# The order of VectorE's steps around rotary rows and score factors, and two buffers for the expert activations, in an encoder layer on one core

## The reference, cut to what matters

```python
def encoder_layer(x, ...):               # x_prompt (1,256,1024) and x_sample (1,512,1024), f32
    h = rms_norm(x, norm1_g)
    proj = h @ w_in                      # six slices of 512 columns and 32 low-rank columns
    gq, gk, gv, gog, glr_f, glr_b, dq, dk, dv = split(proj)
    a = gla_mixer(...)                   # 4 heads, chunked gated linear attention, forward and backward
    d = diff_attention(...)              # 4 heads; q = apply_rope(rms_norm(q)), k likewise
    x = x + concat(a, d) @ w_out
    h2 = rms_norm(x, norm2_g)
    return x + expert_choice_ffn(h2, ...)  # 16 experts, each takes its own 2*n/16 tokens

def apply_rope(x):                       # first half times cos minus second times sin, and so on
    return concatenate([x1*cos - x2*sin, x2*cos + x1*sin], axis=-1)

# gated linear attention, one head and direction, b the running sum of the log gates in a chunk of 64
scores = (q * exp(b - b_mid)) @ (k * exp(b_mid - b)).T     # masked, then times v

# one expert: xe its rows, 2048 hidden columns
ye = (silu(xe @ w_gate) * (xe @ w_up)) @ w_down * gates
out[idx] += ye
```

## Time and profile before

| | us |
|---|---|
| median of 3 runs | 1541.56 (1541.54 to 1542.34) |
| the profiled execution's own time | 1541.64 |
| its span | 1539.8 |
| PE busy | 1503.8 (98%) |
| DVE busy | 1242.6 (81%) |
| ACT busy | 1089.9 (71%) |
| POOL busy | 123.3 (8%) |

### The profile page before, as it was taken

The page is one execution under the profiler, slowest core; times in us unless marked ns, Lnnn a source line. Parts: engine busy times, 40 slices in busy tenths (PEclk is TensorE's granted clock), DMA queues, the critical chain, the costliest instruction groups (busy, mean ns, idle before and its releaser), DMA issues.

```text
span 1539.8 us, 18601 instructions
## 1 busy us (share of the span) xinstructions
PE 1503.8 (98%) x7293; PEld 1228.2 (80%) x7293; DVE 1242.6 (81%) x1133; ACT 1089.9 (71%) x1230; POOL 123.3 (8%) x103
## 2 busy tenths in 40 slices
PE   7999999999989999999999999999999999999997
PEld 6787777678868888888888888888888888888885
DVE  5348678785589898888889888888988888898985
ACT  7456356775457778787777878778777878778784
POOL 1023131000000101000000000010000101000000
PEclk9999999999999999999999999999999999999999
DMA  6111101401759999999999999999999999999992
GB/s 232 56 55 56 38 18 56 152 28 56 273 182 390 367 385 378 395 381 393 376 386 387 376 394 379 393 380 385 384 377 393 379 394 379 387 389 382 393 370 66
DMA packets 191942, 447.98 MB, mean 291 GB/s; under 512 B 12968, under 2 KB 13296, under 8 KB 191856
## 3 DMA queue, kind: packets, MB, share of 16 engines
q1 hardware_dynamic: 187440, 433.03, 75.3%
q0 software_dynamic: 3968, 12.65, 3.5%
q10 hardware_dynamic: 448, 1.12, 0.2%
HBM read 434.19 MB, written 12.58 MB: 290 GB/s over the span
## 4 chain that ended last, share of the span: by engine, by line
PE 89%; DVE 5%; ACT 3%; issue 1%; DMA 1%; POOLq 0%; POOL 0%; SPq 0%; ACTq 0%; DVEq 0%
PE ps L920 23%; PE ps L922 23%; PE ps L921 23%; PE ps L593 5%; PE ps L595 4%; PE ps L594 4%; PE ps L955 1%; PE ps L809 1%; PE ps L843 1%; DVE states L1456 1%; DVE slice_low L1370 1%; PE ps L913 1%; DMA slice_raw<-in_w_in 1%; ACT yr L1071 1%; DVE t L1487 1%
## 5 line engine op out<-in xcount | busy, mean ns | idle before, releaser
L1781 DVE TENSOR_TENSOR wl<-raw,wh 128x2048 fp32r<-128x2048 f32 x384 | 873.5, 2291 | 125.5 <-ACT wh L1305 123.8
L1305 ACT CAST wh<-raw 128x2048 fp32r<-128x2048 f32 x384 | 731.2, 1913 | 125.0 <-PE ps L922 122.8
L920 PE MATMUL ps<-wh,XTh 128*128 128x512 f32 x1024 | 405.4, 396 | 0.9 <-issue 0.9
L922 PE MATMUL ps<-wl,XTh 128*128 128x512 f32 x1024 | 400.0, 391 | 0.0
L921 PE MATMUL ps<-wh,XTl 128*128 128x512 f32 x1024 | 399.1, 390 | 0.0
L922 PEld LDWEIGHTS ps<-wl,XTh 128*128 128x128 f32 x1024 | 192.3, 188 | 41.0
L920 PEld LDWEIGHTS ps<-wh,XTh 128*128 128x128 f32 x1024 | 192.4, 188 | 38.8 <-issue 1.1
L921 PEld LDWEIGHTS ps<-wh,XTl 128*128 128x128 f32 x1024 | 192.6, 188 | 38.0
L920 PE MATMUL ps<-wh,gTh 128*128 128x512 f32 x512 | 201.1, 393 | 1.2 <-DVE gTl L1792 1.2
L922 PE MATMUL ps<-wl,gTh 128*128 128x512 f32 x512 | 199.7, 390 | 0.0
L921 PE MATMUL ps<-wh,gTl 128*128 128x512 f32 x512 | 199.4, 389 | 0.0
(11 more groups left out here) (244 smaller groups left out, 1553.6 us busy)
## 6 DMA issues: line engine op xcount, KB each, us to landing
raw<-in_w_gate SPq DMA_DIRECT2D x128, 1024.0 KB, 10.5
raw<-in_w_up SPq DMA_DIRECT2D x128, 1024.0 KB, 10.5
raw<-in_w_down SPq DMA_DIRECT2D x128, 1024.0 KB, 10.6
slice_raw<-in_w_in SPq DMA_DIRECT2D x6, 2048.0 KB, 8.0
X<-in_x_sample SPq DMA_DIRECT2D x8, 512.0 KB, 12.2
slice_raw<-in_w_out SPq DMA_DIRECT2D x2, 2048.0 KB, 9.2
X<-in_x_prompt SPq DMA_DIRECT2D x4, 512.0 KB, 4.4
h_rows<-hn SPq DMA_DIRECT2D x4, 512.0 KB, 3.3
```

Of the source, the lines that this page charges most:

```text
L920: pe.matmul(out, hi, rhs_h, start=first, stop=False)
L922: return pe.matmul(out, hi, rhs_l, start=False, stop=last)
L1305: act.copy(wh[:, n % CONV, :], raw[:, n % RAW, :]).then_inc(s_wh, 1)
L1781: dve.tensor_tensor(wl[:, n % CONV, :], raw[:, n % RAW, :], wh[:, n % CONV, :].bitcast(F32), ALU.subtract).then_inc(s_wl, 1)
```

## The change

Four edits.

1. **Body loop, DVE's list.** At t = 4 `score_factors(h + 1)` goes from the end of the step to its front. At t = 2 `cosine_half` and `rope_add` of the previous row go in front of `sum_squares`. At t = 5 `cosine_half` of the previous row goes in front of the first four low parts, and `rope_add` behind the last four, ahead of `inverse_roots`. Other steps keep their order, and so do all other engines in this loop.
2. **Own buffers for the last expert's last activations.** gTh and gTl become pairs; the second is used by q = 63 alone (`act_buffer`).
3. **The turning of q = 63** goes from behind both tiles of down 62 to between them, on PE, and ACT's and DVE's `turned(63)` one place forward with it. POOL clears the spare columns of the second pair too (two more memsets), and PE waits for three such marks and not two.
4. **`add_rows` on POOL** waits for the previous addition first, and for the new rows behind that.

```diff
-        gTh = at("gTh", 180224, [P, FC, P], F32R)
-        gTl = at("gTl", 182272, [P, FC, P], F32R)
+        gTh = [at("gTh0", 180224, [P, FC, P], F32R), at("gTh1", 186368, [P, FC, P], F32R)]
+        gTl = [at("gTl0", 182272, [P, FC, P], F32R), at("gTl1", 200704, [P, FC, P], F32R)]
...
+        def act_buffer(q):
+            return 1 if q == NQ - 1 else 0
...
             def add_rows(e):
+                if e >= 1:
+                    pool.wait_ge(s_add, 32 * e)
                 pool.wait_ge(s_y, 2 * (e + 1))
                 if e == NE - 1:
                     pool.wait_ge(s_ylast, 2)
-                if e >= 1:
-                    pool.wait_ge(s_add, 32 * e)
...
-            pool.memset(gTh[:, :, CAP:P].bitcast(F32), 0.0)
-            pool.memset(gTl[:, :, CAP:P].bitcast(F32), 0.0).then_inc(s_pad, 1)
+            for j in range(2):
+                pool.memset(gTh[j][:, :, CAP:P].bitcast(F32), 0.0)
+                pool.memset(gTl[j][:, :, CAP:P].bitcast(F32), 0.0).then_inc(s_pad, 1)
...
                 use_tile(place["d", q, 0])
+                if q == NQ - 2:
+                    turn_hidden(NQ - 1)
                 use_tile(place["d", q, 1])
...
-            pe.wait_ge(s_pad, 2)
+            pe.wait_ge(s_pad, 3)
...
-            turn_hidden(NQ - 1)
             down(NQ - 1)
...
-                if n == place["d", NQ - 1, 0]:
+                if n == place["d", NQ - 2, 1]:
                     turned(NQ - 1)          # on ACT, and the same on DVE
...
                 turning = t == NT - 1 and h + 1 < HEADS
+                if t == 4 and h + 1 < HEADS:
+                    score_factors(h + 1)
                 if turning:
+                    if rotary(i - 1) is not None:
+                        cosine_half(rotary(i - 1))
                     low_parts(FIRST + h + 1, range(0, 4))
+                if t == 2 and rotary(i - 1) is not None:
+                    cosine_half(rotary(i - 1))
+                    rope_add(rotary(i - 1))
                 if v is not None:
                     sum_squares(v)
                 if turning:
                     low_parts(FIRST + h + 1, range(4, KD))
-                if rotary(i - 1) is not None:
+                    if rotary(i - 1) is not None:
+                        rope_add(rotary(i - 1))
+                if t not in (2, NT - 1) and rotary(i - 1) is not None:
                     cosine_half(rotary(i - 1))
                 if v is not None:
                     inverse_roots(v)
-                if rotary(i - 1) is not None:
+                if t not in (2, NT - 1) and rotary(i - 1) is not None:
                     rope_add(rotary(i - 1))
...
-                if t == 4 and h + 1 < HEADS:
-                    score_factors(h + 1)
```

More of the change, by code:

```diff
@@ L942, in use_tile @@
                         d = slice(half * 512, (half + 1) * 512)
-                        mm = products(ps[:, 4 + half, :], (gTh[:, ff, :], gTl[:, ff, :]),
+                        mm = products(ps[:, 4 + half, :], (gTh[act_buffer(q)][:, ff, :], gTl[act_buffer(q)][:, ff, :]),
                                       h_[:, f, d], l_[:, f, d], s == 0 and ff == 0,
@@ L1324, in turned @@
                 act.wait_ge(s_hT, q + 1)
-                act.copy(gTh[:, :, 0:CAP], ps[:, 6, 0:FC * CAP].rearrange("p (f c) -> p f c", f=FC)).then_inc(s_gth, 1)
+                act.copy(gTh[act_buffer(q)][:, :, 0:CAP], ps[:, 6, 0:FC * CAP].rearrange("p (f c) -> p f c", f=FC)).then_inc(s_gth, 1)
             act.wait_ge(s_op, 2 * NT)
@@ L1791, in turned @@
                 dve.wait_ge(s_gth, q + 1)
-                dve.tensor_tensor(gTl[:, :, 0:CAP], ps[:, 6, 0:FC * CAP].rearrange("p (f c) -> p f c", f=FC),
-                                  gTh[:, :, 0:CAP].bitcast(F32), ALU.subtract).then_inc(s_gtl, 1)
+                dve.tensor_tensor(gTl[act_buffer(q)][:, :, 0:CAP], ps[:, 6, 0:FC * CAP].rearrange("p (f c) -> p f c", f=FC),
+                                  gTh[act_buffer(q)][:, :, 0:CAP].bitcast(F32), ALU.subtract).then_inc(s_gtl, 1)
             dve.wait_ge(s_issued, 1)
```

## The result

| | before | changed |
|---|---|---|
| median, us | 1541.71 (1541.37 to 1542.61) | 1544.61 (1544.24 to 1545.41) |
| span of the profiled execution | 1539.8 | 1542.4 |

19 runs each. The ratio is 1.0019, with a 95% interval of 1.0012 to 1.0025: the change makes the kernel 2.9 us slower, for a forecast of 2.8. The interval does not contain 1.0, so the kernel is slower clear of noise. The prediction had said that a change of under 0.2% can't be told from none; these runs do tell one of 0.19%.

A forecast was written before the change was run, and what follows sets the result against it. PE bounds the expert loop, two thirds of the time; the change acts on PE's waits in two body-loop windows and at the end. 2 x 2.1 - 1.4 = +2.8 gives a 1544.3 us median, range 1543.5 to 1545.4.

The forecast's parts named there:

- The end: Turning of the last hidden rows, placed between two tiles: 0.59 us in place of 1.99, so 1.4 us gained.
- Both covers: At the end: hidden rows ready 0.2 us before PE's turning; DVE's low half done at 1522.74, wanted about 1523.1.
- t = 2, chain 0.7 later: DVE at step 2: the way to ACT and back is uncovered, so `sums` and what follows come 0.7 us later.
- Bank of step 5's unit: PE's unit of step 5 waits for ACT's scaling of row 3 and starts at 134.44, 0.7 us later.
- the gain: PE's 0.9 us won at its first rotary transposes, claimed to be waited away at step 5's unit.
- t = 4, the clash: POOL's product comes between DVE's two score factors; the second takes 2.60 us, not 0.95, both together 3.47.
- the window: Rotary stretch of the body loop through PE's unit of step 7, occurring twice; forecast 2.1 us later each time.
- DVE kept the pair: Rival at t = 4: POOL does not come between DVE's products; 1.5 us lost per window, 1543.1 in all; chance 0.17.
- t = 5 and on: Low parts take 3.52 to 3.67 us; step 7's unit waits for row 5's scaling, net 2.1 us later per window.
- the waits simply go: Rival: PE's 2.4 us of waits vanish in each window, 6.2 us faster in all, 1535.4; chance 0.16.
- the windows come out even: Rival: equal waits replace the old ones in each window, only the end's gain is left, 1540.2; chance 0.10.
- more is lost behind step 7: Rival: lateness at step 7 also delays `carry` and the next head, 3 us or more a window, 1546 or above; chance 0.11.

The follow-up runs named there:

- e1: The turning between the tiles and the last expert's own buffers alone, body loop and wait order as in the kernel before: 1540.38 against 1541.68 us.
- e3: The kernel before with only the t = 2 move, cosine half and rope add ahead of the sum of squares: 1543.28 against 1541.68 us.
- e7: The changed kernel with t = 2 ordered sum of squares, cosine half, rope add, inverse roots: 1543.21 us against 1541.71 for the kernel before.
- e6: The changed kernel with POOL's key product held until DVE's two score factors are done: 1543.95 us against 1541.71 for the kernel before.
- e2: The kernel before with only DVE's new order in the body loop, at t = 2, 4 and 5: 1546.01 against 1541.68 us.
- e5: The kernel before with only the t = 5 moves, cosine half ahead of low parts, rope add ahead of inverse roots: 1542.27 against 1541.71 us.
- e4: The kernel before with only the score factors moved to the front of t = 4: 1544.29 against 1541.68 us.
- e8: The changed kernel, DVE reordered: inverse roots after rope add (t = 2), before cosine half (t = 3); second score factor behind rope add (t = 4): 1538.96 against before's 1541.71 us.
- e9: e8 with the inverse roots ahead of the cosine half at t = 4 too: 1538.30 us against 1541.78 for the kernel before.

## Why the prediction was right

- **The end, -1.4:** 0.59 in place of 1.99 in the trace, and -1.3 in e1. Both covers held: the hidden rows are ready at 1523.65 and PE turns them at 1524.01; in e1 the low half is done at 1522.68, and PE has no wait for it. The two added memsets stand ahead of a wait for the same DMA on POOL as before.
- **t = 2, chain 0.7 later:** `sums` 0.8 later from the step's start. The forecast was 0.7: it let the rope add start 0.71 behind the cosine half, and it starts 0.79 behind. Alone the move costs 1.6 (e3), and with the way to ACT covered 1.4 of it is back (e7). This is the best shown step: added alone and taken away alone, with the same size.
- **Bank of step 5's unit:** 134.13, with ACT's scaling as the releaser, which the list before did not have at all. From the first transposes it is 18.53 us, before it was 17.82: 0.7 later, as forecast. Two readings behind it were wrong. The 0.17 us between scaling and unit before was not "just the hand-over": where PE does wait for ACT, 0.05 us pass (134.08 to 134.13), so 0.12 was slack, and the scaling itself came 0.83 later. And the gain was not lost there, but one wait earlier, at row 2, which the forecast had not looked at. Neither wait is on the chain, so the sum did not hang on them: it followed DVE and ACT, and that path was right.
- **t = 4, the clash:** the second product took 2.60 as read from step 10. The rope add of row 3 had PE waiting 1.69 (forecast: over 1.5). By the forecast the window would be 0.6 shorter if DVE kept the pair; in e6, the nearest case, it was 0.3 to 0.4 shorter (37.49 - 37.10 in the trace, 0.33 by the runs). In e6 POOL's product starts at 137.60, 0.15 after the end of the second factor at 137.45, a hand-over that the forecast for this case had left out, and the cosine half behind it comes as much later. In the rival POOL would have been waiting already; if the hand-over falls away there, the estimate is 0.39 + 0.15 = 0.54, so the 0.6 was somewhat large. It stood in a bound and a rival, not in the sum.
- **t = 5 and on:** the low parts took 3.67, and the unit of step 7 came 2.11 later, for 2.1 forecast. The forecast had it wait for ACT's scaling of row 5, and so it does: no wait is listed in front of 153.09, but the unit starts 0.05 behind the scaling's end and 0.73 behind the first key transpose. The same 0.73 or 0.74 stands in e2, e5, e6 and e7, which have the new order at t = 5, and 0.60 in the kernel before and in e1, e3, e4, e8 and e9, which have the old one.
- **Luck in the last digit:** measured from the first transposes, the scaling of row 3, the second factor's end and the scaling of row 5 all came 0.12 to 0.14 later than forecast. The hand-over from ACT to PE was 0.05 where 0.14 stood in the sum. The two nearly cancel. With the hand-over right the forecast would have been 2.0 a window, for 2.11 measured.
- **The share of the two single moves** was not asked of the prediction, but they interact: the windows of e3, e4 and e5 grow by 2.39 us in sum, that of e2, with all three, by 2.14. Where in the window the 0.25 goes stays open.

The rivals: that the waits simply go is refuted by e3 and e4, which each remove the wait in question and are slower; that the windows come out even, by e2; that DVE keeps the pair, by the row at 136.46. That more is lost behind step 7 is out too: from there to the second window's first transposes it is 58.00 us (153.09 to 211.09), before 57.95. The forecast had given its own range 0.46, so more than half lay with the others.

## What to carry to other kernels

A wait that the profile names is only the first one in line. Before moving the work that ends it, see whether the waiting engine is on the chain at all (here PE was not, from 120 to 150 us), look for the next things that it needs (here the next rope add, and a bank freed only 0.12 us before PE needed it) and for what the moved work covered (here a way to another engine and back of 0.6 us beyond the sum). Where one instruction is held up anyway, put the short chain that another engine waits for in front of it. In e9 this one move gave 0.7 us, while each move that ended a named wait made the window longer (e3, e4, e5).

## What the runs showed of the hardware that was not expected

When POOL's product with operands in SBUF becomes ready while the first of two such products of DVE runs, POOL goes next, and DVE's second one waits for the whole of it: 2.60 or 2.61 us in place of 0.95, at step 4 (changed kernel, e4) as at step 10 of the kernel before. I had given 0.17 to the other outcome. Holding POOL back does not remove the cost but hands most of it to the next such product of DVE (e6: 2.02 in place of 0.69, so 1.33 of the 1.65 us); about 0.4 a window came back.
